# The down product of an ffn as seven half products

## The chip, the core and the metric

The kernel runs on one core of a Trainium2 chip. The number is device time in microseconds (us) of one execution, lower is better. TensorE multiplies 128x128 tiles into PSUM banks of 512 float32 columns; VectorE, ScalarE and GpSimd work on SBUF (GpSimd not on PSUM); SyncE issues the transfers between HBM and SBUF.

## The reference, cut to what matters

Two transformer blocks on 1024 tokens of width 1024. The change lies in the last part of the first block:

```python
u = rmsnorm(h, ffn_norm_pre)
gt = causal_dwconv(u @ ffn_w_gate, ffn_conv_w, ffn_conv_b)          # 1024 -> 2816
y = (gelu(gt) * (u @ ffn_w_up)) @ ffn_w_down                        # 2816 -> 1024
h = h + rmsnorm(y, ffn_norm_post)
```

The product with `ffn_w_down` is [1024 tokens, 2816] x [2816, 1024]. Everything is float32. A float32 product is made of three fp32r ones: each operand is split into a rounded high part and the rest (low), and high x high, high x low and low x high are added in PSUM.

## The kernel before, in words

The kernel is a row of stages; each is a block in which the five engines run their own lists of instructions, joined by semaphores, with a barrier at its end. Two stages matter here.

`stage_ffn` (L1329) makes the inner rows, tile by tile (22 tiles of 128 features, `KF` = 22), and SyncE stores each to HBM (`hid_d`, "inner_scratch", L1417). Tiles 3 to 20 are made with seven half products in place of eight (`seven`, L1508): sums of weights by VectorE (`combine`, L1762), high parts by ScalarE (L1595), low parts of weights by GpSimd (L1442). The last tile is plain: TensorE's last matmuls there are L1582, then VectorE multiplies (`multiply(KF - 1)`, L1849, L1759) and SyncE stores. Near its end SyncE loads the first two K tiles of the down weights and of the rows (L1431, L1434), ScalarE makes the first high part (L1676), GpSimd its low part (L1466).

`stage_down` (L1852) computes the down product transposed: the output is 8 tiles of 128 features by 1024 tokens, in two halves of 512 tokens. In a half all eight banks (one for each output tile) gather over the 22 K tiles. A step is one K tile: SyncE loads 128 weight rows of 1024 (L1875) and 128 inner rows of 512 tokens (L1877), two steps ahead; ScalarE casts the high parts (L1950, L1951); VectorE subtracts the low parts (L1924, L1925), and `lo_made` releases TensorE's 8 x 3 matmuls (L1892 to L1894); the end of the step (`used`) releases ScalarE's next cast. Between the halves VectorE copies the banks to `y` (L1930), and TensorE's second half waits for each bank's copy (L1890). ScalarE squares `y` (L1959), GpSimd adds the squares into `acc` (L1987), and TensorE multiplies by ones for the sums over features (L1913, L1915). The next stage (`stage_in2`, L1998) starts with the inverse root of these sums (L2200); `end_part` (L3957) clears semaphores between them.

## Time and profile before

| | |
|---|---|
| median of 3 runs | 2900.97 us (2899.46 to 2901.78) |
| the profiled execution | 2906.65 us, its span 2904.6 us |
| TensorE matmuls busy over the span | 2715.2 us (93%) |
| VectorE, ScalarE, GpSimd busy | 1827.6, 1249.0, 655.7 us |
| the ffn stage's seven-product tiles | 19.4 us each, 18 of them |
| the down stage, first to last matmul | 1254.9 to 1505.1 us of the span |

A line of the profile's order of time gives the start, the duration, the engine, the line, the operation with the tiles it writes and reads, its count, and in brackets how long the engine had been idle before it and what ended that. TensorE's matmuls overlap, so a matmul's duration is longer than the distance to the next; the distances give the pace. The granted clock (PEclk) is a share of full speed.

### The profile page before, as it was taken

The page shows a single profiled execution, that of the slowest core. Times are in us where ns is not written, and L with a number is a line of the kernel's source. Part 1 is how long each engine was busy: PE and PEld are TensorE (multiplying, and loading weights), DVE is VectorE, ACT ScalarE, POOL GpSimd, SP SyncE. Part 2 cuts the span into 40 slices and gives each one's busy share as a digit, 9 for nine tenths or more (in the row PEclk, how much of TensorE's full clock was granted, in tenths as well). Part 3 has the DMA queues.
Part 4 walks back from the last instruction along what each step waited for, and adds up shares of the span by engine and source line. Part 5 has one row for each costly group of instructions (what it writes and reads, how often), then busy time and mean ns, then how long its engine had stood idle before and what let it go on. Part 6 is the DMA issues. An engine that isn't in the chain of part 4 may idle for free. (4 is left out here: it accounts for less than half of the span.)

```text
span 2904.6 us, 38465 instructions
## 1 busy us (share of the span) xinstructions
PE 2715.2 (93%) x14472; PEld 2350.3 (81%) x14472; DVE 1827.6 (63%) x2284; ACT 1249.0 (43%) x1870; POOL 655.7 (23%) x406
## 2 busy tenths in 40 slices
PE   8989999999879999999989998889998999999993
PEld 7989999899768888878767888667786688888882
DVE  5366655462487777733434733765354899999996
ACT  4342333332333233222334213654333477777773
POOL 3000000002165555500110000003510144444441
PEclk9999999999999999999989999889998999999997
DMA  5343233343212222235432211113303599999996
GB/s 190 99 130 99 85 102 99 120 141 128 87 44 66 88 87 69 92 115 196 140 99 87 52 58 59 44 44 109 94 25 131 215 416 420 414 416 412 416 414 236
DMA packets 254404, 460.34 MB, mean 158 GB/s; under 512 B 22818, under 2 KB 181810, under 8 KB 229186
## 3 DMA queue, kind: packets, MB, share of 16 engines
q1 hardware_dynamic: 244770, 423.95, 40.7%
q0 software_dynamic: 9504, 34.61, 3.0%
q8 instruction: 88, 1.44, 0.2%
q14 instruction: 42, 0.34, 0.0%
HBM read 387.08 MB, written 71.43 MB: 158 GB/s over the span
## 5 line engine op out<-in xcount | busy, mean ns | idle before, releaser
L3889 DVE TENSOR_TENSOR k_w_lo<-k_raw,k_w_hi 128x2048 fp32r<-128x2048 f32 x192 | 433.6, 2288 | 34.5 <-ACT k_w_hi L3825 30.9
L3825 ACT CAST k_w_hi<-k_raw 128x2048 fp32r<-128x2048 f32 x192 | 363.1, 1911 | 64.4 <-PE bank L3743 41.3
L120 PE MATMUL bank<-u_hi,p_w_hi 128*128 128x342 f32 (+2 forms) x720 | 237.8, 330 | 8.9 <-DVEq L889 6.0
L121 PE MATMUL bank<-u_lo,p_w_hi 128*128 128x342 f32 (+2 forms) x720 | 231.9, 322 | 0.0
L122 PE MATMUL bank<-u_hi,p_w_lo 128*128 128x342 f32 (+2 forms) x720 | 231.6, 322 | 0.0
L3741 PE MATMUL bank<-k_w_hi,k_x_hi 128*128 128x512 f32 x512 | 203.0, 397 | 1.3 <-DVE k_x_lo L3895 1.0
L3743 PE MATMUL bank<-k_w_hi,k_x_lo 128*128 128x512 f32 x512 | 199.8, 390 | 0.0
L3742 PE MATMUL bank<-k_w_lo,k_x_hi 128*128 128x512 f32 x512 | 199.3, 389 | 0.0
L1471 PE MATMUL bank<-u_ffn_hi,f_w_hi 128*128 128x512 f32 (+3 forms) x520 | 171.4, 330 | 17.6 <-DVE f_inner L1759 8.4
L1472 PE MATMUL bank<-u_ffn_lo,f_w_hi 128*128 128x512 f32 (+3 forms) x520 | 167.7, 323 | 0.0
L1473 PE MATMUL bank<-u_ffn_hi,f_w_lo 128*128 128x512 f32 (+3 forms) x520 | 167.4, 322 | 0.0
L1924 DVE TENSOR_TENSOR f_w_lo<-d_raw,f_w_hi 128x1024 fp32r<-128x1024 f32 x43 | 53.6, 1247 | 156.5 <-ACT d_x_hi L1951 156.5
L1892 PE MATMUL bank<-d_x_hi,f_w_hi 128*128 128x512 f32 x352 | 139.5, 396 | 8.4 <-DVE qa L1930 4.5
L120 PEld LDWEIGHTS bank<-u_hi,p_w_hi 128*128 128x128 f32 x720 | 136.9, 190 | 9.4 <-DVEq L889 6.3
L1044 POOL TENSOR_TENSOR f_w_lo<-d_raw,f_w_hi 128x1024 fp32r<-128x1024 f32 x2 | 5.0, 2499 | 611.3 <-ACT f_w_hi L1117 611.3
L1442 POOL TENSOR_TENSOR f_w_lo<-f_raw,f_w_hi 128x512 fp32r<-128x512 f32 x66 | 107.6, 1632 | 141.2 <-ACT f_w_hi L1595 141.2
L1893 PE MATMUL bank<-d_x_lo,f_w_hi 128*128 128x512 f32 x352 | 139.1, 395 | 0.0
L1894 PE MATMUL bank<-d_x_hi,f_w_lo 128*128 128x512 f32 x352 | 138.8, 394 | 0.0
L121 PEld LDWEIGHTS bank<-u_lo,p_w_hi 128*128 128x128 f32 x720 | 137.0, 190 | 0.0
L122 PEld LDWEIGHTS bank<-u_hi,p_w_lo 128*128 128x128 f32 x720 | 136.7, 190 | 0.0
L857 DVE COPY_PREDICATED h_scores<-level,bank 128x512 f32<-128x512 int32 x72 | 53.3, 741 | 128.9 <-PE bank L769 102.6
L1442 POOL TENSOR_TENSOR f_w_lo<-d_raw,f_w_hi 128x512 fp32r<-128x512 f32 x72 | 104.5, 1453 | 84.9 <-ACT f_w_hi L1595 84.8
(606 smaller groups left out, 7354.9 us busy)
## 6 DMA issues: line engine op xcount, KB each, us to landing
k_raw<-in_w_e_gate_dram SPq DMA_DIRECT2D x64, 1024.0 KB, 7.0
k_raw<-in_w_e_up_dram SPq DMA_DIRECT2D x64, 1024.0 KB, 7.6
k_raw<-in_w_e_down_dram SPq DMA_DIRECT2D x64, 1024.0 KB, 8.2
d_raw<-in_ffn_w_down_dram SPq DMA_DIRECT2D x44, 512.0 KB, 3.6
p_w<-in_w_in_dram SPq DMA_DIRECT2D x34, 512.0 KB, 4.4
f_raw<-in_ffn_w_gate_dram SPq DMA_DIRECT2D x22, 512.0 KB, 3.7
f_raw<-in_ffn_w_up_dram SPq DMA_DIRECT2D x22, 512.0 KB, 4.9
inner_scratch<-f_inner SPq DMA_DIRECT2D x22, 512.0 KB, 5.5
```

What stands on the lines that cost most here:

```text
L120: pe.matmul(out, wh[:, t, :], xh[t][:, c:c + n], start=t == 0, stop=False)
L121: pe.matmul(out, wh[:, t, :], xl[t][:, c:c + n], start=False, stop=False)
L122: m = pe.matmul(out, wl[:, t, :], xh[t][:, c:c + n], start=False, stop=t == tiles - 1)
L1442: pool.tensor_tensor(ring(wl, q), operand(q)[0], ring(wh, q), ALU.subtract).then_inc(lo_made, 1)
L1471: pe.matmul(out, ring(wh, q)[:, k, :], xh, start=first, stop=False)
L1472: pe.matmul(out, ring(wh, q)[:, k, :], xl, start=False, stop=False)
L1473: return pe.matmul(out, ring(wl, q)[:, k, :], xh, start=False, stop=last)
L3741: pe.matmul(out, hi, wh[:, q, col], start=first, stop=False)
L3742: pe.matmul(out, hi, wl[:, q, col], start=False, stop=False)
L3743: return pe.matmul(out, lo, wh[:, q, col], start=False, stop=last)
L3825: act.copy(wh[:, q, :], raw[:, r, :]).then_inc(hi_made, 1)
L3889: dve.tensor_tensor(wl[:, q, :], raw[:, r, :], wh[:, q, :], ALU.subtract).then_inc(lo_made, 1)
```

## The change

The down product is written as a 2x2 block product: K in two halves of 11 tiles (the first digit of a weight block's name and of a row block's), output features in two halves of 512 (the second digit of the weights'), tokens in two halves of 512 (the second digit of the rows'). It is made with seven products of half size in turn instead of eight. A product multiplies one sum or single block of weights by one of rows (`COMBOS`), in 11 steps of 4 x 3 matmuls, into four banks; the other four are emptied meanwhile. VectorE makes the sums, and the rows' low parts; the weights' low parts are made by VectorE in products 0, 1 and 6 and by GpSimd in 2 to 5. Results are added and subtracted in `y` by VectorE (`fold`), after a copy by ScalarE where a quarter of `y` is written first. Block 11 of the weights and of the rows is loaded once into kept buffers, later block 00. Operands have rings of 4 (weights, loads) and 5 (rows). Steps 0 and 1 are made ready in `stage_ffn`, whose last multiply and store move to `stage_down`. `h` is loaded by tiles in product 5. Twelve of the sixteen squares are added by GpSimd during the product, the last four by TensorE. The sums' banks are 4 and 5 now. The loops are unrolled. The diff is cut to its core; of `stage_down` the new lists are shown, and the class `Down` holds the rings, the loads and the splits.

```diff
                 if n == KF - 1:
-                    sp.wait_ge(lo_made, first_operand(KF - 1))
-                    for s in range(2):
-                        sp.dma_start(down_raw[:, s, :], A["ffn_w_down"][0][s * P:(s + 1) * P, :]).then_inc(down_in[s], 16)
-                    for s in range(2):
-                        sp.wait_ge(hid_out[s], 16)
-                        sp.dma_start(down_x[s], hid_d[s][:, 0:BANK]).then_inc(down_in[s], 16)
+                    raw_read(sp, n - 1)
+                    sp.wait_ge(pmm, PRODUCTS * len(FAST) - 1)
+                    down.load(sp, 0)
+                    down.load(sp, 1)
                 store(n - 1)
-            store(KF - 1)
+            raw_read(sp, KF - 1)
+            down.load(sp, 2)
+            down.load(sp, 3)
...
             keep_gate(KF - 1)
-            act.wait_ge(down_in[0], 32)
-            act.copy(wh[:, 1, :, :].rearrange("p k n -> p (k n)"), down_raw[:, 0, :]).then_inc(down_hi, 1)
-            gelu(KF - 1)
+            for step in range(2):
+                down.weights_high(act, step)
+                down.rows_high(act, step)
+            act.wait_ge(conv3, KF)
+            act.activation(part[:, (KF - 1) % 2, 0:SEQ], part[:, (KF - 1) % 2, 0:SEQ], ACT.Gelu_apprx_tanh).then_inc(down.tail_gelu, 1)
...
             multiply(KF - 2)
+            dve.wait_ge(lo_made, first_operand(KF - 1))
+            down.sums(dve, 0)
+            down.sums(dve, 1)
             conv(KF - 1)
-            multiply(KF - 1)
+            for step in range(2):
+                down.weights_low(dve, step)
+                down.rows_low(dve, step)
...
+HALF_K = KF // 2
+COMBOS = (
+    (("10", "11", ALU.subtract), ("10", "11", ALU.add)),
+    (("00", "11", ALU.add), ("00", "11", ALU.add)),
+    (("00",), ("01", "11", ALU.subtract)),
+    (("00", "10", ALU.add), ("11",)),
+    (("11",), ("10", "00", ALU.subtract)),
+    (("01", "11", ALU.add), ("00",)),
+    (("01", "00", ALU.subtract), ("00", "01", ALU.add)),
+)
+KEPT_W = ("11",) * 6 + ("00",)
+KEPT_X = ("11",) * 4 + ("00",) * 3
+STEPS = PRODUCTS * HALF_K
+LOW_BY_DVE = (0, 1, 6)
...
+    def transfers(self, step):
+        i, j = divmod(step, HALF_K)
+        at = 0
+        out = []
+        for name in COMBOS[i][0][:2]:
+            if name != KEPT_W[i]:
+                out.append((self.piece(step, at), self.weights(name, j)))
+                at += 1
+        for name in COMBOS[i][1][:2]:
+            if name != KEPT_X[i]:
+                out.append((self.piece(step, 1), self.rows(name, j)))
+        if i == 0:
+            out.append((self.kept_w[j], self.weights(KEPT_W[0], j)))
+            out.append((self.kept_x[j], self.rows(KEPT_X[0], j)))
+        if i == 4:
+            out.append((self.kept_x[j], self.rows(KEPT_X[4], j)))
+        ahead = step - (5 * HALF_K + 5)
+        if 0 <= ahead < HALF_K:
+            out.append((self.kept_w[ahead], self.weights(KEPT_W[6], ahead)))
+        return out
...
+    def weights_ready(self, engine, step):
+        made = self.w_lo_dve if self.by_dve(step) else self.w_lo_pool
+        engine.wait_ge(made, sum(self.by_dve(n) == self.by_dve(step) for n in range(step + 1)))
+
+    def load(self, sp, step):
+        if step >= 4:
+            self.weights_ready(sp, step - 4)
+            sp.wait_ge(self.x_lo, step - 3)
+        if step < HALF_K:
+            n = HALF_K + step
+            sp.wait_ge(self.hid_out[n % 2], 16 * (n // 2 + 1))
+        for to, source in self.transfers(step):
+            sp.dma_start(to, source).then_inc(self.w_in[step % 4], 16)
...
+    def sums(self, dve, step):
+        i = step // HALF_K
+        dve.wait_ge(self.w_in[step % 4], self.landed(step))
+        if self.is_sum(step, 0):
+            a, b, op = COMBOS[i][0]
+            if step >= 2:
+                self.weights_ready(dve, step - 2)
+            dve.tensor_tensor(self.t[step % 2], self.weight_source(a, i, step, 0), self.weight_source(b, i, step, 1), op).then_inc(self.t_made, 1)
+        if self.is_sum(step, 1):
+            a, b, op = COMBOS[i][1]
+            if step >= 2:
+                dve.wait_ge(self.x_lo, step - 1)
+            dve.tensor_tensor(self.s[step % 2], self.row_source(a, i, step), self.row_source(b, i, step), op).then_inc(self.s_made, 1)
...
+        if step >= 4:
+            act.wait_ge(self.used, step - 3)
+        elif step >= 2:
+            act.wait_ge(self.tail_mm, 1)
+        act.copy(self.ring(self.wh, step).rearrange("p k n -> p (k n)"), self.weight_raw(step)).then_inc(self.w_hi, 1)
...
+        if step >= 5:
+            act.wait_ge(self.used, step - 4)
+        act.copy(self.xh[step % 5], self.row_raw(step)).then_inc(self.x_hi, 1)
...
+    def weights_low(self, engine, step):
+        made = self.w_lo_dve if self.by_dve(step) else self.w_lo_pool
+        engine.wait_ge(self.w_hi, step + 1)
+        engine.tensor_tensor(self.ring(self.wl, step).rearrange("p k n -> p (k n)"), self.weight_raw(step),
+                           self.ring(self.wh, step).rearrange("p k n -> p (k n)"), ALU.subtract).then_inc(made, 1)
+
+    def rows_low(self, dve, step):
+        dve.wait_ge(self.x_hi, step + 1)
+        dve.tensor_tensor(self.xl[step % 5], self.row_raw(step), self.xh[step % 5], ALU.subtract).then_inc(self.x_lo, 1)
...
+            d.load(sp, 4)
+            d.load(sp, 5)
+            sp.wait_ge(tail_made, 2)
+            sp.dma_start(d.hid_d[KF - 1], part[:, last, 0:SEQ]).then_inc(d.hid_out[last], 16)
+            for step in range(6, STEPS):
+                if step == HALF_K:
+                    sp.wait_ge(d.hid_out[0], 16 * HALF_K)
+                d.load(sp, step)
+                k = step - 5 * HALF_K
+                if 0 <= k < KD:
+                    sp.dma_start(h[:, k, :], h_load[:, k, :]).then_inc(h_in, 16)
+            sp.wait_ge(h_in, 16 * KD)
...
+            for step in range(STEPS):
+                i, j = divmod(step, HALF_K)
+                wh, wl = d.ring(d.wh, step), d.ring(d.wl, step)
+                xh, xl = d.xh[step % 5], d.xl[step % 5]
+                d.weights_ready(pe, step)
+                pe.wait_ge(d.x_lo, step + 1)
+                for p in range(4):
+                    if j == 0:
+                        free_bank(i, p)
+                    out = bank_of(i, p)[:, :]
+                    pe.matmul(out, wh[:, p, :], xh, start=j == 0, stop=False)
+                    pe.matmul(out, wh[:, p, :], xl, start=False, stop=False)
+                    m = pe.matmul(out, wl[:, p, :], xh, start=False, stop=j == HALF_K - 1)
+                    if j == HALF_K - 1:
                         m.then_inc(mm, 1)
+                if j < HALF_K - 1:
+                    m.then_inc(d.used, 1)
                 else:
+                    pe.wait_ge(mm, 4 * (i + 1))
+                    pe.sem_inc(d.used, 1)
+            pe.wait_ge(added, 12)
+            pe.wait_ge(folded, 28)
             for half in range(2):
+                pe.matmul(bank[4 + half][:, :], K["ones"][:, :], acc[:, half * BANK:(half + 1) * BANK], start=True, stop=half == 0)
+            for p in range(4):
+                pe.wait_ge(squared, 12 + p + 1)
+                pe.matmul(bank[5][:, :], K["ones"][:, :], sqs[:, p, :], start=False, stop=p == 3)
...
+            dve.wait_ge(d.tail_gelu, 1)
+            dve.wait_ge(d.tail_mm, 1)
+            for j, (c, w) in enumerate(SEQS):
+                half = part[:, last, c:c + w]
+                dve.tensor_tensor(half, half, bank[UP_LAST[j]][:, 0:w], ALU.mult).then_inc(tail_made, 1)
+            for step in range(2, STEPS + 1):
+                if step < STEPS:
+                    d.sums(dve, step)
+                if step > 2:
+                    if d.by_dve(step - 1):
+                        d.weights_low(dve, step - 1)
+                    d.rows_low(dve, step - 1)
+                i, j = divmod(step, HALF_K)
+                if 4 <= j < 8 and i:
+                    evict(i - 1, j - 4)
+            for p in range(4):
+                evict(PRODUCTS - 1, p)
...
+            for step in range(2, STEPS):
+                d.weights_high(act, step)
+                d.rows_high(act, step)
+                i, j = divmod(step, HALF_K)
+                if 4 <= j < 8 and i in (1, 2, 3, 5):
+                    c, t = {1: (0, 0), 2: (1, 1), 3: (0, 1), 5: (1, 0)}[i]
+                    copy(c, t, j - 4, i - 1)
+                if 7 <= j and i in (4, 5, 6):
+                    square(4 * (i - 4) + j - 7)
+            for n in range(12, 16):
+                square(n)
...
+            for step in range(2, STEPS):
+                if not d.by_dve(step):
+                    d.weights_low(pool, step)
+                i, j = divmod(step, HALF_K)
+                if 8 <= j and i in (4, 5, 6):
+                    add(4 * (i - 4) + j - 8)
+                if j == 0 and i in (5, 6):
+                    add(4 * (i - 4) - 1)
+            add(11)
```

The folds (`evict`), by product: 1 into quarter (0, 0); 2 into (1, 1); 3 into (0, 1) and (0, 0); 4 into (0, 0); 5 into (1, 0) and (1, 1); 6 into (1, 1). Each is four instructions of 128x512 that read a bank and `y`. `raw_read`, `ring` and `hid_out` are those of `stage_ffn`.

## Rows read from the trace of the kernel before

**Rows 1.** The page's first line.
```profile
span 2904.6 us, 38465 instructions
```
**Rows 2.** Busy time by stretch: PE, PEld, DVE, ACT, POOL, PEclk, DMA share, GB/s.
```profile
1195.80:1215.20 19.40, 19.40 (x109) 17.02 (x109) 14.91 (x17) 5.86 (x11) 10.60 (x8) 1.00 0.25 82
...
1226.00:1252.00 26.00, 25.16 (x134) 22.39 (x132) 13.14 (x12) 5.45 (x8) 6.05 (x3) 1.00 0.05 21
1252.00:1380.00 128.00, 122.89 (x528) 101.11 (x528) 39.89 (x45) 35.09 (x45) 0.00 (x0) 0.97 0.52 172
```
**Rows 3.** Order of time, TensorE: down stage's start, one K tile, middle, end.
```profile
1250.77 0.39 PE L1473 MATMUL bank<-u_ffn_hi,f_w_lo 128*128 128x512 f32 x1
1254.89 0.79 PE L1892 MATMUL bank<-d_x_hi,f_w_hi 128*128 128x512 f32 x1 [3.73 <-DVE d_x_lo L1925]
...
1261.30 0.39 PE L1892 MATMUL bank<-d_x_hi,f_w_hi 128*128 128x512 f32 x1
...
1265.42 0.39 PE L1892 MATMUL bank<-d_x_hi,f_w_hi 128*128 128x512 f32 x1
...
1270.86 0.39 PE L1892 MATMUL bank<-d_x_hi,f_w_hi 128*128 128x512 f32 x1
...
1382.30 0.76 PE L1892 MATMUL bank<-d_x_hi,f_w_hi 128*128 128x512 f32 x1 [4.52 <-DVE qa L1930]
...
1504.72 0.39 PE L1894 MATMUL bank<-d_x_hi,f_w_lo 128*128 128x512 f32 x1
```
**Rows 4.** Order of time, TensorE in the ffn stage: shorter waits, what followed.
```profile
824.72 0.42 PE L1471 MATMUL bank<-u_ffn_hi,f_w_hi 128*128 128x342 f32 x1 [1.20 <-POOL u_ffn_lo L1446]
...
877.97 0.39 PE L1471 MATMUL bank<-u_ffn_hi,f_w_hi 128*128 128x258 f32 x1 [2.18 <-POOL f_w_lo L1442]
...
878.44 0.28 PE L1471 MATMUL bank<-u_ffn_hi,f_w_hi 128*128 128x258 f32 x1
...
879.65 0.42 PE L1472 MATMUL bank<-u_ffn_lo,f_w_hi 128*128 128x258 f32 x1
```
**Rows 5.** Order of time, VectorE and ScalarE at the change of stages.
```profile
1251.27 1.29 DVE L1759 TENSOR_TENSOR f_inner<-f_inner,bank 128x512 f32<-128x512 f32 x2 [4.29 <-PE bank L1473]
...
1253.49 0.62 ACT L1951 CAST d_x_hi<-f_raw 128x512 fp32r<-128x512 f32 x1 [5.42 <-SPq L1356]
```
**Rows 6.** By tile (ns: least, median, most); order of time, four back to back.
```profile
L1951 ACT CAST d_x_hi<-f_raw x44: 612/619/619, 1253.5 to 1495.2; 128x512 fp32r<-128x512 f32 x44
L1925 DVE TENSOR_TENSOR d_x_lo<-f_raw,d_x_hi x44: 681/684/1777, 1254.1 to 1497.0; 128x512 fp32r<-128x512 f32 x44
...
860.88 2.49 DVE L1727 TENSOR_TENSOR f_sums<-f_parts,f_sums 128x512 fp32r<-128x512 f32 x4
```
**Rows 7.** Order of time: VectorE beside GpSimd, reading a bank, then SBUF alone.
```profile
1221.39 0.69 DVE L1792 TENSOR_TENSOR f_parts<-bank,f_parts 128x512 f32<-128x512 f32 x1
1221.42 1.29 POOL L1442 TENSOR_TENSOR f_w_lo<-f_raw,f_w_hi 128x512 fp32r<-128x512 f32 x1 [1.43 <-ACT f_w_hi L1595]
...
1383.63 11.78 POOL L1987 TENSOR_TENSOR ka<-ka,d_sq 128x512 f32<-128x512 f32 x7
...
1387.38 1.78 DVE L1925 TENSOR_TENSOR d_x_lo<-f_raw,d_x_hi 128x512 fp32r<-128x512 f32 x1
```
**Rows 8.** Transfers: KB each and us to landing; SyncE's issue (ns); GB/s in 40 slices.
```profile
k_raw<-in_w_e_gate_dram SPq DMA_DIRECT2D x64, 1024.0 KB, 7.0
...
f_raw<-inner_scratch SPq DMA_DIRECT2D x42, 256.0 KB, 3.7
...
L1877 SPq DMA_DIRECT2D f_raw<-inner_scratch x42: 332/333/765, 1256.4 to 1487.5; - x42
...
GB/s 190 99 130 99 85 102 99 120 141 128 87 44 66 88 87 69 92 115 196 140 99 87 52 58 59 44 44 109 94 25 131 215 416 420 414 416 412 416 414 236
```
**Rows 9.** Order of time: a product with ones, and the next stage's first work.
```profile
1505.45 1.10 PE L1913 MATMUL bank<-ka,ones 128*128 128x512 f32 x2 [0.34 <-POOL ka L1987]
...
1516.12 1.26 ACT L168 ACTIVATE va<-bank,eps 128x512 f32<-128x512 f32 x2 [7.39 <-PEq L3960]
```

More of the change, by code:

```diff
@@ L1355, in stage_ffn @@
     rstd, token = g, acc
[L1356 to L1358 removed]
+    with nc.Block() as block:
         def ring(b, q):
@@ new lines, in stage_down, with quarter, bank_of @@
+def stage_down(nc, ctx, K, bank, d, part, y, acc, sqs, h, h_load):
+    mm, copied, folded, squared, added, h_in, tail_made = sems(ctx, nc, "d", "mm copied folded squared added h_in tail_made")
+    UP_LAST = (4, 5)
+    last = (KF - 1) % 2
+    def quarter(c, t, p):
+        return y[4 * c + p][:, t * BANK:(t + 1) * BANK]
+    def bank_of(i, p):
+        return bank[4 * (i % 2) + p]
+    SQUARES = tuple((c, t, p) for c, t in ((0, 1), (0, 0), (1, 0), (1, 1)) for p in range(4))
+    with nc.Block() as block:
@@ L1904, in _ @@
-                step(half, 1, 1)
-                with pe.Fori(1, PAIRS_K - 1) as i:
-                    for s in range(2):
-                        step(half, 2 * i + s, s)
-                step(half, KF - 2, 0)
-                step(half, KF - 1, 1, last=True)
-            for half in range(2):
-                pe.wait_ge(kept, KD + half + 1)
-                pe.wait_ge(added, KD if half == 0 else 2 * KD - 1)
-                pe.matmul(bank[half][:, :], K["ones"][:, :], acc[:, half * BANK:(half + 1) * BANK], start=True, stop=half == 0)
@@ L1921, in low @@
-            def low(half, k, s, made=False):
-                dve.wait_ge(hi_made, KF * half + k + 1)
-                if not made:
-                    dve.tensor_tensor(wl[:, 1 - s, :], raw[:, s, :], wh[:, 1 - s, :], ALU.subtract)
-                dve.tensor_tensor(xl[:, s, :], xr[s], xh[:, s, :], ALU.subtract).then_inc(lo_made, 1)
-            def keep(half):
-                for j in range(KD):
-                    dve.wait_ge(mm, KD * half + j + 1)
-                    dve.tensor_copy(y[j][:, half * BANK:(half + 1) * BANK], bank[j][:, :]).then_inc(kept, 1)
```

246 lines of the change are left out of this document (132 added, 114 removed).

## The prediction, made before the change was run

> **What bounds the kernel now.** The order of reading was: the span, then the busy time by stretch, then TensorE's own order of time, then the waits of the other engines around it. The profiled execution has a span of 2904.6 us [rows 1] and took 2906.65 us; the median of the runs shown is 2900.97 us. In the down stage TensorE is busy 122.9 of 128 us in the first half, VectorE 39.9, ScalarE 35.1 and GpSimd not at all [rows 2]. So TensorE bounds this stage, and its order of time says by what. Two matmuls that are one K tile (24 matmuls) apart start 5.44 us apart, which is 0.2267 us for each matmul of 512 columns [rows 3]. The stage has 22 x 8 x 3 x 2 = 1056 of them, 239.4 us at that pace. From the end of the last matmul of the stage before (1250.77 + 0.39 = 1251.16) to the end of the last one here (1504.72 + 0.39 = 1505.11) are 253.95 us [rows 3]. The 14.5 us between are two interruptions: 3.73 us idle at the start and 4.52 us at 1382.30, when the second half's banks wait for their copies [rows 3]. Behind the first one 15 matmuls take 1261.30 - 1254.89 = 6.41 us instead of 3.40, a pace of 0.427 us: this is the lower of the two clock levels (1.2 GHz), and the granted clock is 0.97 over that half [rows 2, 3]. I count 3.0 us for that after each of the two gaps; 239.4 + 3.7 + 3.0 + 4.5 + 3.0 = 253.7, so the stage is explained to 0.3 us. From 1505.11 to the first work of the next stage at 1516.12 are another 11.0 us [rows 3, 9].
>
> **Matmuls removed.** Seven products of 11 steps with 4 x 3 matmuls are 924, 132 fewer. Shape and type are as before, so 132 x 0.2267 = 29.9 us go, all of it on the path.
>
> **Start of the stage.** Before, the gap holds the barrier (ScalarE is released at 1253.49 by SyncE, about 0.6 us after the store that followed the two multiplies beginning at 1251.27) and then the cast and low part of the first rows [rows 5]. Now steps 0 and 1 are split inside the stage before, and the last multiply and store come after the barrier. TensorE waits only for the barrier: I take 0.7 us, bounds 0.5 and 1.5. What hides the moved work (four sums and four low parts on VectorE, 4.8 us, four casts on ScalarE, 2.5 us) is the end of the stage before: of its last 26 us VectorE is busy 13.1, ScalarE 5.5 and GpSimd 6.1 [rows 2]. Without that cover it would cost 4.8 us at the start. The loads of steps 0 to 3 go on SyncE's queue ahead of two stores, which nobody awaits soon. That saves 3.0 us of gap. A wait of 1.20 us was followed by no slow stretch (342 columns in 0.42 us for the first matmul, as after other waits), one of 2.18 us was followed by matmuls of 258 columns in 0.42 us instead of 0.28 [rows 4], so 0.7 us should not cost the clock and the 3.0 us of slow matmuls go as well.
>
> **Middle.** The eight copies between the halves are replaced by copies and folds of four banks at a time while the other four are filled, with eleven steps between; nothing is left to wait at. VectorE's folds of product i stand behind its low parts of step 4 and later of product i + 1, and those need operands that TensorE frees only after product i, so VectorE never waits there with something queued behind. Saved: 4.5 + 3.0 = 7.5 us.
>
> **New drains.** At each product's end TensorE waits for its own last matmul before it releases the operands. A matmul lasts 0.39 us at a pace of 0.227 [rows 3], so 0.16 us plus a semaphore; 0.2 x 6 = 1.2 us lost, bounds 0 and 0.4 x 6 = 2.4.
>
> **The first product and its transfers.** A step now lasts 12 x 0.2267 = 2.72 us, and in product 0 each step loads four pieces of 256 KB (two go to buffers kept for later): 1.05 MB in 2.72 us is 385 GB/s. The experts hold 412 to 420 GB/s [rows 8], and their 1024 KB pieces of the gate's weights (512 columns) are rows of 2 KB like these, so the rate is there, barely. The ring is tighter than the rate. Load s + 4 waits for the low rows of step s; then come four issues at 0.33 us busy each [rows 8], some 1.9 us with their spacing, and a landing of 3.7 us for one 256 KB piece alone. Then VectorE passes two rounds of four instructions before the low rows of s + 4 are there. Each takes 0.60 us back to back (four in 2.49 us, the last one's tail included) [rows 6], so 4.8 us: 1.9 + 3.7 + 4.8 + some latencies = 10.7, four steps in 10.9 us of matmuls. SyncE's one new wait, for the tail multiply, stands ahead of the store and load 6, and is over before load 5 is issued. Steps 0 to 3 are loaded before the barrier and step 2 waits for the tail multiply: 1.3 us [rows 5] and four instructions and more, ready about 5 us after the barrier, when TensorE needs it at 5.4. I follow it with pieces that queue behind each other at 2.5 us a step and find step 5 about 0.5 us late and the later ones 0.2: 1.5 us lost, bounds 0 and, with a landing of 7.0 us as the experts' 1024 KB have [rows 8], (1.9 + 7.0 + 4.8) / 4 = 3.4 us a step, 0.7 x 7 = 5 us, and with a gap that reaches 2 us another 3 for the clock: 8.
>
> **VectorE and GpSimd in each step.** In products 0, 1 and 6 VectorE has four instructions, 2.4 us of 2.72; in products 2 to 5 it has two (1.2 us) and GpSimd one of 1.29 us [rows 6, 7]. ScalarE has two of 0.62 us [rows 6], and up to two more in some steps (2.4 us): no bound. The row that matters is the meeting of the two engines. A low part of VectorE that met GpSimd's additions took 1.78 us instead of 0.68 [rows 6, 7]; one that reads a bank took 0.69 us right beside a GpSimd instruction of 1.29 us, which wasn't longer either [rows 7]. So folds are free of it, and splits and sums are not. Counted as exclusive time, products 2 and 3 need 22 x 0.62 + 11 x 1.29 = 27.8 us of 29.9, product 4 with three additions 31.7, product 5 with four 33.0. Product 6 has 44 x 0.62 = 27.3, its 8 folds 5.0, and additions of which up to 4.4 us hit: 32.3 to 36.7. That is 7.3 to 11.7 us over in products 4 to 6. The rings let VectorE lead TensorE by three steps less its own 2.7 us: 5.5 us. A tile of the ffn stage had 14.9 us of VectorE and 10.6 us of GpSimd in 19.4 us, 25.5 together, and TensorE never waited [rows 2]; this speaks for the low end. I take 3.0 us, bounds 0 and 12.7 (each event of those products adding its full 0.65 or 1.1 us to VectorE: 20.7, less 2.5 won back and 5.5 of lead). The loads of h (512 KB each, eight, in product 5) add to one or two small transfers a step and stay far under the rate; the 3 us that they could cost is inside these bounds.
>
> By the Trainium skill (SBUF — State Buffer, Who interferes with whom) a VectorE instruction with two SBUF inputs and a GpSimd instruction that reads SBUF exclude each other for a whole instruction, while one with at most one SBUF input is free. The trace agrees: 1.78 against 0.68 us, and 0.69 us for the bank's. Taken strictly it speaks against putting weights' splits on GpSimd, and its result is the first rival below.
>
> **Tail.** Before, GpSimd's backlog of additions keeps the sum product waiting 4.52 us and more. Now twelve of sixteen squares are added during the product and the last four go straight to TensorE. Six products with ones instead of three, 1.10 us each at full clock less overlap [rows 9], bounds 0.85 and 1.9, are 6.0 us; VectorE's last fold and ScalarE's last square (0.7 + 0.6) lie beside the first two. With 0.2 ahead and 1.3 behind for the stage change: 7.5 us instead of 11.0, so 3.5 saved, bounds -2 and 4.5.
>
> **Sum.** 29.9 + 3.0 + 3.0 + 7.5 + 3.5 - 1.2 - 1.5 - 3.0 = 41.2 us. The profiled execution would go from 2906.65 to 2865.5, the median from 2900.97 to 2859.8, about 2860 us.
>
> **Rivals.** (1) The two engines exclude each other and nothing overlaps: 12.7 instead of 3.0, 2869.5 us. For it: the 1.78 us row. Against: the ffn tile without a wait. Chance 0.15. (2) Product 0 is bound by its transfers: 8 instead of 1.5, 2866 us. For: 385 of 415 GB/s and a ring of four. Against: the 3.7 us landing. Chance 0.12. (3) Slower: if each VectorE instruction of products 2 to 5 meets GpSimd, a step is 2 x 1.7 = 3.4 us, and if TensorE's short waits there bring the clock down, it runs at 12 x 0.427 = 5.1 us for 44 steps: 2.4 x 44 = 106 us, 2966 us. It decides from 18 such steps on (18 x 2.4 = 43). Against: a wait of 1.20 us left the clock up [rows 4]. Chance 0.03. (4) The product is not what limits, and the time removed is waited for elsewhere (h, or code fetched for an unrolled stage): no gain, 2901 us. The ffn stage ahead is unrolled at the same density and shows no such wait [rows 2]. Chance 0.02.
>
> **How the numbers follow.** The forecast, 2860 us, has the remaining 0.68; its own range is 2853 (every loss zero) to 2866. To leave out no more than 2 in 10 the range goes to the first two rivals, and to both together, 41.2 - 9.7 - 6.5 = 25.0: 2876 us. About 0.2% (6 us) is what a measurement of this kernel can tell from no change. Faster 0.95, same 0.02, slower 0.03.
>
> **What would show it.** Matmuls at 0.227 us in all seven products; a gap under 1 us at the start with no stretch at 0.427 behind; waits on low rows in the first eleven steps of some tenths; the same on VectorE in products 4 to 6, if anywhere; 7 to 8 us from the last product to the next stage. The prediction is wrong if a gap over 2 us stands anywhere inside, or if product 0's steps take 3.4 us.

## The result and the profile after

The changed kernel took 2868.43 us (median of 4 runs, 2861.21 to 2870.06) against 2900.22 us for the kernel before in the same runs: a ratio of 0.9889, 95% interval 0.9875 to 0.9902, or 28 to 36 us less. Forecast were 2860 us and a range up to 2876; without the first two rivals it would have ended at 2866, below the measured median. The profiled execution took 2861.21 us, against the 2906.65 us of the one before [rows 1].

```profile
span 2859.5 us, 38444 instructions
```

These two profiles are 45 us apart, which is more than the change did. I measure the change on the stretch that it touches, called the stage below: from the end of the ffn's last matmul to ScalarE's first work of the next stage (L168). Before it is 1251.16 to 1516.12, 264.96 us [rows 3, 9]; after 1244.39 to 1473.07, 228.68 us. That is 36.3 us less. The other 9 us lie outside the stage, 6.8 ahead of it and some 2 behind. There the kernels differ only in the last ffn tile, where TensorE is busy throughout in both, and in where buffers lie; the times vary from execution to execution (b1_before below).

Busy time by stretch, as in [rows 2]; the stretches are an ffn tile, the ffn's end, product 0, products 1 to 5, product 6:

```profile
1195.80:1215.20 19.40, 19.40 (x110) 17.01 (x110) 13.41 (x16) 5.84 (x10) 10.49 (x8) 1.00 0.16 63
1218.40:1244.40 26.00, 25.99 (x137) 23.09 (x135) 15.21 (x18) 6.58 (x11) 3.00 (x3) 1.00 0.53 182
1244.80:1279.40 34.60, 31.61 (x133) 24.39 (x133) 28.57 (x47) 14.18 (x24) 0.00 (x0) 1.00 0.85 291
1279.40:1432.30 152.90, 151.00 (x661) 123.56 (x662) 130.19 (x153) 75.28 (x135) 75.75 (x52) 1.00 0.64 215
1432.30:1465.60 33.30, 31.08 (x132) 24.24 (x132) 31.74 (x47) 13.71 (x23) 6.40 (x4) 1.00 0.36 118
```

The granted clock is 1.00 throughout, where the first half before had 0.97 [rows 2]. The ffn's end still keeps TensorE busy 25.99 of 26 us with the first two steps' preparation in it. VectorE is busy 31.74 of 33.30 us in product 6.

TensorE's order of time, answering [rows 3]: start, the waits of product 0, two products' ends, two of the four waits of product 6, and the tail (beside [rows 9]):

```profile
1244.00 0.39 PE L1469 MATMUL bank<-u_ffn_hi,f_w_lo 128*128 128x512 f32 x1
1244.86 0.47 PE L2063 MATMUL bank<-d_x,f_w_hi 128*128 128x512 f32 x1 [0.47 <-PEq L1356]
...
1253.62 0.47 PE L2063 MATMUL bank<-d_x,f_w_hi 128*128 128x512 f32 x1 [0.31 <-DVE d_x L2006]
1257.48 0.47 PE L2063 MATMUL bank<-d_x,f_w_hi 128*128 128x512 f32 x1 [0.86 <-DVE d_x L2006]
1261.39 0.47 PE L2063 MATMUL bank<-d_x,f_w_hi 128*128 128x512 f32 x1 [0.90 <-DVE d_x L2006]
1270.30 0.47 PE L2063 MATMUL bank<-d_x,f_w_hi 128*128 128x512 f32 x1 [0.50 <-DVE d_x L2006]
...
1278.65 0.39 PE L2065 MATMUL bank<-d_x,f_w_lo 128*128 128x512 f32 x1
1279.35 0.47 PE L2063 MATMUL bank<-d_x,f_w_hi 128*128 128x512 f32 x1 [0.30 <-PE bank L2065]
...
1340.50 0.47 PE L2063 MATMUL bank<-d_x,f_w_hi 128*128 128x512 f32 x1 [0.44 <-PE bank L2065]
...
1449.22 0.47 PE L2063 MATMUL bank<-d_x,f_w_hi 128*128 128x512 f32 x1 [0.47 <-DVE d_x L2006]
1452.93 0.47 PE L2063 MATMUL bank<-d_x,f_w_hi 128*128 128x512 f32 x1 [0.72 <-DVE d_x L2006]
...
1466.02 1.95 PE L2076 MATMUL bank<-mixed_squares,ones 128*128 128x512 f32 x4 [0.34 <-DVE vm L2084]
```

The two long interruptions are gone: 0.47 us at the start where 3.73 stood, nothing in the middle where 4.52 stood. In their place are many short ones of three kinds. At 1279.35 and 1340.50 TensorE waits for its own last matmul. The waits up to 1270 lie in product 0, those from 1449 on in product 6, both on VectorE's low parts. What VectorE itself waits for in product 0 (what, for whom, us in total, times, longest) is a transfer:

```profile
DVE d_raw L1971 <- DMA d_kept<-inner_scratch: 5.9, 5, 1.4
```

From a product's first matmul to the next one's, with 132 x 0.2267 = 29.92 us as the least (all 924 matmuls are in these traces). Product 6 is taken to the start of its last matmul and 0.2267 us more. Tail is from the end of the last matmul to L168, and whole time the median of the runs with the ratio's 95% interval to the kernel before in the same runs:

```
kernel          product 0  products 1 to 5               6      tail  stage   whole time, ratio
before          -          -                             -      11.0  264.96  2900.97
b1_before       -          -                             -      10.8  264.45  2896.63, 0.9975 to 1.0
changed         34.49      30.51 30.64 30.62 30.47 30.60 33.34  7.38  228.68  2868.43, 0.9875 to 0.9902
e1_again        35.35      30.47 30.62 30.59 30.49 30.61 33.54  7.35  229.65  2868.36, 0.9862 to 0.9898
e2_no_drain     32.63      29.92 29.92 29.92 29.92 29.92 34.78  6.80  224.45  2864.10, 0.9853 to 0.9886
e3_early        33.59      30.49 30.59 30.58 30.48 30.59 33.86  7.35  228.16  2865.16, 0.986 to 0.9893
e4_no_adds      35.37      30.51 30.62 30.59 30.49 30.61 31.90  7.06  227.78  2866.80, 0.985 to 0.989
e5_all_dve      34.18      30.49 30.60 30.58 30.47 30.64 33.40  7.06  228.05  2863.61, 0.9849 to 0.9899
e6_all_pool     33.55      32.46 32.34 30.58 30.51 31.13 33.33  7.06  231.59  2868.79, 0.9871 to 0.9918
e7_three        33.07      29.92 29.92 29.92 29.92 29.92 35.25  6.52  225.08  2859.85, 0.9845 to 0.9889
e8_store_late   32.11      30.48 30.60 30.58 30.47 30.59 34.66  7.38  227.50  2866.99, 0.9865 to 0.9919
e9_dve_alone    32.71      29.92 29.92 29.92 29.92 29.92 32.58  6.51  222.04  2856.13, 0.9837 to 0.9871
e10_h_ahead     32.26      29.92 29.92 29.92 29.92 29.92 32.16  6.51  221.20  2857.31, 0.984 to 0.9868
e11_gap         35.03      30.48 32.98 32.22 30.47 30.62 33.28  7.35  233.06  2865.40, 0.9853 to 0.9901
```

The intervals of the whole time are some 10 us wide and most overlap; the causes are therefore read from the product lengths, which agree to 0.1 us in products 1 to 5. Product 0 agrees less: changed, e1_again, e4_no_adds, e5_all_dve and e11_gap have the same code there and take 34.18 to 35.37 us.

### The profile page after: what moved, and what is told of

Its sections match the earlier page's. It is cut to its first block and busy times, and to the rows that moved or that the text cites. A ratio compares the mean times of both kernels' runs of the same rounds, so it can differ in the third digit from the quotient of the medians.

```text
span 2859.5 us, 38444 instructions
## 1 busy us (share of the span) xinstructions
PE 2677.1 (94%) x14346; PEld 2315.4 (81%) x14346; DVE 1927.9 (67%) x2433; ACT 1276.8 (45%) x1952; POOL 711.8 (25%) x446
## 5 line engine op out<-in xcount | busy, mean ns | idle before, releaser
L4008 ACT CAST k_w_hi<-k_raw 128x2048 fp32r<-128x2048 f32 x192 | 363.1, 1912 | 64.2 <-PE bank L3926 41.2
L2063 PE MATMUL bank<-d_x,f_w_hi 128*128 128x512 f32 x308 | 121.2, 394 | 7.5 <-DVE d_x L2006 5.2
L3883 POOL DMA_INDIRECT y_scratch<-k_y,k_to x32 | 73.8, 2308 | 213.9 <-POOLq L3881 213.9
L1467 PEld LDWEIGHTS bank<-u_ffn_hi,f_w_hi 128*128 128x128 f32 x520 | 99.9, 192 | 27.5 <-issue 14.4
L2065 PE MATMUL bank<-d_x,f_w_lo 128*128 128x512 f32 x308 | 120.0, 390 | 0.0
```

Source lines behind the costliest of these rows:

```text
L1467: pe.matmul(out, ring(wh, q)[:, k, :], xh, start=first, stop=False)
L4008: act.copy(wh[:, q, :], raw[:, r, :]).then_inc(hi_made, 1)
```

## Experiments

### The same two kernels again

b1_before is the kernel before, e1_again the changed kernel, each unchanged.

> The kernel before once more, to see how much of the difference between two profiled executions lies outside the down stage. Its first profile has 265.0 us from the last ffn matmul to the next stage's first work. Theory A (the stage is the same each time): 265 within 1 us again, so the stage saves 35 to 36 us, and what is left over, up to 6 us either way, is spread elsewhere. Theory B (the first profile had an unusually slow stage): 262 or less, which would bring the stage's saving to the 32 us of the medians.

> The changed kernel again, to tell the stage's saving from what differs between executions. From the end of the last ffn matmul to the first work of the stage after the down product the changed kernel's profile has 228.7 us, the kernel before 265.0: 36.3 us saved there, while the two profiled executions differ by 45 us and the medians by 32. Theory A (the stage is the same in each execution, the rest is spread of stages that were not touched): again 228.7 within 1 us, and a time ratio of 0.987 to 0.990. Theory B (the stage itself varies, since its short waits sometimes bring the clock down): another stage length, 232 us or more, with a stretch of matmuls 0.427 us apart.

The stages are 264.45 and 229.65 us, 34.8 apart after 36.3 in the first pair: each is within 1 us of the first time. What lies ahead of the stage moves more: it begins at 1251.16 and 1242.99 us in the two executions of the kernel before and at 1244.39 and 1249.83 in those of the changed one, so both have both. One place of it can be named, the wait on GpSimd in the ffn of [rows 4], which in both kernels is 2.1 to 2.2 us in the late executions and 1.0 to 1.1 in the early ones; totals of TensorE's waits in the ffn, the kernel before first and b1_before second:

```profile
PE bank L1471 <- POOL f_w_lo L1442: 2.2, 1, 2.2
```
```profile
PE bank L1471 <- POOL f_w_lo L1442: 1.0, 1, 1.0
```

Behind the longer wait (2.10 to 2.18 us in before, e1_again, e2_no_drain and e5_all_dve) 15 matmuls of 258 columns start 0.21 to 0.22 us apart; behind the shorter one (0.98 in b1_before, 1.06 in the changed kernel) all keep their 0.12. That is some 1.5 us more, and with the wait it covers the 2.2 us that arise in the ffn between the two executions of the kernel before. The other 6.0 of their 8.2 us are there already at the ffn's first matmul (774.0 and 768.0) and were not followed.

Inside the stage the two interruptions are not the same twice. Starts of TensorE's matmuls in b1_before, each gap and the first matmul back at full pace:

```profile
1246.72 0.75 PE L1892 MATMUL bank<-d_x_hi,f_w_hi 128*128 128x512 f32 x1 [3.73 <-DVE d_x_lo L1925]
...
1250.24 0.40 PE L1894 MATMUL bank<-d_x_hi,f_w_lo 128*128 128x512 f32 x1
...
1373.79 0.77 PE L1892 MATMUL bank<-d_x_hi,f_w_hi 128*128 128x512 f32 x1 [5.46 <-DVE qa L1930]
...
1379.90 0.40 PE L1894 MATMUL bank<-d_x_hi,f_w_lo 128*128 128x512 f32 x1
```

Behind the same 3.73 us of gap as before, 8 distances take 3.52 us, which is 1.7 us lost to slow matmuls instead of 3.0; behind the second gap, 5.46 us for 4.52, 14 take 6.11, 2.9 us lost instead of 2.5. All four together are 13.8 us here and 13.7 in the first execution: the sums agree although the parts do not.

### The drain between products

```diff
-                else:
-                    pe.wait_ge(mm, 4 * (i + 1))
-                    pe.sem_inc(d.used, 1)
```

ScalarE, which is what that signal releases, waits for `mm` itself at those steps.

> TensorE no longer waits for its own last matmul at a product's end; the operands of that step are released to ScalarE by the semaphore of its last matmuls themselves. In the changed kernel's profile products 1 to 5 last 30.5 to 30.6 us instead of 29.9. Theory A (the 0.6 us is this drain: about 0.4 idle and 0.2 of lost overlap): products 1 to 5 last 29.9 to 30.0, the stage 225.0, 3.7 us less. Theory B (the 0.6 us belongs to the change of banks or to operands that come late): products last 30.5 as before and the stage keeps 228.7.

Products 1 to 5 fall from 30.47 to 30.64 to exactly 29.92 each. The boundary of products 0 and 1 has no mark of its own in TensorE's order of time of e2_no_drain:

```profile
1284.23 0.39 PE L2073 MATMUL bank<-d_x,f_w_lo 128*128 128x512 f32 x1
1284.46 0.39 PE L2071 MATMUL bank<-d_x,f_w_hi 128*128 128x512 f32 x1
1284.68 0.39 PE L2072 MATMUL bank<-d_x,f_w_hi 128*128 128x512 f32 x1
```

So a drain costs 0.55 to 0.72 us. Starts are 0.70 us apart at 1278.65 in the changed kernel's rows above and the next two (1279.35 and 1279.65) 0.30 apart, in place of twice 0.227. Of these 0.55 us 0.30 are the idle time in brackets, 0.16 the unfinished end of the last matmul, and the rest the slower first one. Where the idle time is 0.41 or 0.44 the whole is 0.67 to 0.72. The six idle times are 2.2 us together. Six drains are 3.8 us, and a seventh stands ahead of the tail (6.80 instead of 7.35). But product 6 grows from 33.3 or 33.5 to 34.8: a part of what TensorE wins it loses to VectorE there.

### Product 0: releasing loads earlier, and the store

e3_early releases the loads by the sums that consumed the piece, and no longer by the low parts made from them:

```diff
-            self.weights_ready(sp, step - 4)
-            sp.wait_ge(self.x_lo, step - 3)
+            for side, made, low in ((0, self.t_made, None), (1, self.s_made, self.x_lo)):
+                if self.is_sum(step - 4, side):
+                    sp.wait_ge(made, self.count(step - 4, side))
```

(where a side is a single block, the old wait stays). e8_store_late has this and moves the store of the ffn's last row from behind load 5 to behind load 7.

> A load's buffer is released by the sums that read it, where both operands of the step are sums (products 0, 1 and 6), not by the low parts made one round later: 2.4 us and more earlier. In the changed kernel product 0 lasts 34.5 us, of which 29.9 are matmuls and 0.6 its drain. Theory A (the ring's round trip of issue, landing and two rounds of VectorE is what is late): product 0 comes to 30.5 to 31.5 us, the stage to 225.2. Theory B (the transfers' rate, 1.05 MB in each 2.72 us, is what is late): product 0 keeps 34 us or more, its transfers at 400 GB/s before and after.

> Loads released by the sums, as in the run before of that kind, and besides the store of the last inner row (512 KB) is issued behind the loads of step 7 instead of step 5. In that run TensorE still waited 1.62 us at step 4 or 5 and 0.90 us at the next, and while the store was under way the transfers moved 180 to 260 GB/s at a busy share of 0.84 to 0.87. Theory A (the store takes transfer time from the loads of steps 5 and 6): these waits fall to under 1 us together, product 0 from 33.6 to 32 us or less, as far as step 10, which needs the stored row, isn't late then. Theory B (the loads of steps 4 and 5 are late because they start only after the barrier, whatever follows them): the 1.6 us wait stays.

In e3_early the waits of the later steps are gone and the two early ones stay as they were, so it lands between its two theories; e8_store_late shrinks those to 0.8 us together, as its theory A had it. TensorE's waits in product 0, e1_again, e3_early and e8_store_late:

```profile
1263.02 0.47 PE L2063 MATMUL bank<-d_x,f_w_hi 128*128 128x512 f32 x1 [1.56 <-DVE d_x L2006]
1266.92 0.47 PE L2063 MATMUL bank<-d_x,f_w_hi 128*128 128x512 f32 x1 [0.92 <-DVE d_x L2006]
1276.10 0.47 PE L2063 MATMUL bank<-d_x,f_w_hi 128*128 128x512 f32 x1 [0.76 <-DVE d_x L2006]
1279.56 0.47 PE L2063 MATMUL bank<-d_x,f_w_hi 128*128 128x512 f32 x1 [0.49 <-DVE d_x L2006]
```
```profile
1263.25 0.47 PE L2068 MATMUL bank<-d_x,f_w_hi 128*128 128x512 f32 x1 [1.62 <-DVE d_x L2011]
1267.13 0.47 PE L2068 MATMUL bank<-d_x,f_w_hi 128*128 128x512 f32 x1 [0.90 <-DVE d_x L2011]
```
```profile
1262.06 0.47 PE L2069 MATMUL bank<-d_x,f_w_hi 128*128 128x512 f32 x1 [0.22 <-DVE d_x L2011]
1271.07 0.47 PE L2069 MATMUL bank<-d_x,f_w_hi 128*128 128x512 f32 x1 [0.58 <-DVE d_x L2011]
```

The stage begins at the same time in both (1249.97 and 1249.96). Busy time by stretch of e3_early, then of e8_store_late (DMA share and GB/s are the last two):

```profile
1254.00:1258.00 4.00, 4.00 (x19) 3.34 (x18) 3.27 (x7) 1.93 (x4) 0.00 (x0) 1.00 0.86 220
1258.00:1270.00 12.00, 9.48 (x41) 7.13 (x41) 8.34 (x14) 3.67 (x6) 0.00 (x0) 1.00 1.04 402
```
```profile
1254.00:1258.00 4.00, 4.00 (x19) 3.34 (x18) 3.02 (x6) 1.74 (x4) 0.00 (x0) 1.00 0.88 274
1258.00:1270.00 12.00, 11.78 (x51) 9.17 (x51) 9.80 (x17) 4.71 (x9) 0.00 (x0) 1.00 1.05 406
```

In the first four microseconds shown, the transfers move 220 GB/s with the 512 KB store among them and 274 without; both have 402 or 406 afterwards. The store itself does not lower the rate: e8_store_late issues it at 1258.66, and the transfers move 405 GB/s from there to 1262.70. What it takes is its own 512 KB, and with the store moved TensorE's wait at step 4 falls from 1.62 to 0.22 us and the one at step 5 goes. Why the rate is low in those first microseconds, with the store or without, stays open.

Product 0 goes 35.35, 33.59, 32.11 in the three. Executions differ too much to give each step its price from this. The loads of e2_no_drain are those of the changed kernel, its product 0 takes 32.63 us, or some 33.2 with the drain, and it has no waits behind step 5 either. Counted with a drain, the six executions with the changed kernel's loads and store are at 33.2, 34.2, 34.5, 35.0 and twice 35.4 (e6_all_pool, whose low parts of product 0 are made elsewhere, is left out). The two with early loads (e3_early, e7_three) are at 33.6, and the three with early loads and the late store at 32.1 to 33.3. Both edits point the right way by about 1 us each; that the early release alone helps is not shown.

The early release has a limit that can be read: with it the pieces land 6.4 to 7.5 us after their issue (medians of the four kinds) where e1_again has 5.2 to 6.1, at 402 GB/s. They are issued earlier and queue longer. In e8_store_late product 6 takes 34.66 instead of 33.86: why a store in product 0 should matter there was not followed.

### Product 6: additions, lead, or VectorE itself

e4_no_adds leaves out four squares (8 to 11) and the additions in product 6, so a part of the sum of squares is missing. e5_all_dve and e6_all_pool change who makes the weights' low parts:

```diff
-LOW_BY_DVE = (0, 1, 6)
+LOW_BY_DVE = (0, 1, 2, 3, 4, 5, 6)
```
```diff
-LOW_BY_DVE = (0, 1, 6)
+LOW_BY_DVE = ()
```

> The squares of one quarter of y (features 512 to 1023, first 512 tokens) and their four additions on GpSimd are left out, so no GpSimd addition falls into product 6 from its step 8 on; the normalisation of these tokens misses half of its sum. Product 6 lasts 33.3 us in the changed kernel. Theory A (three additions hold up a VectorE instruction by 1.1 us each, 1.78 for 0.68): product 6 comes to 29.9 to 30.4, the stage to 225.4. Theory B (VectorE's four instructions a step and its eight folds alone use up its lead, 26.5 + 4.8 = 31.3 us against 29.9): product 6 keeps 31.5 us or more.

> VectorE makes the weights' low parts in all seven products, GpSimd only adds squares. Theory A (the two engines exclude each other in products 2 to 5: in the changed kernel's product 5 five VectorE instructions in a row start 1.70 us apart instead of 0.60, each beside a GpSimd one, so VectorE enters product 6 with 1.2 us of lead instead of 5.5): a step of products 2 to 5 needs three times 0.60 instead of 2 x 0.60 + 1.29 of shared time, VectorE enters product 6 three steps ahead, and product 6 comes from 33.5 to 30.5 us or less; stage 226.5 or less against 229.7 of the changed kernel run again. Theory B (VectorE has too much to do in product 6 whatever the lead): product 6 stays at 33 us or more.

> GpSimd makes the weights' low parts in all seven products. Theory A (they exclude each other): in products 0, 1 and 6 a step needs 3 x 0.60 + 1.29 = 3.1 us of shared time against 2.72, with the folds and additions of product 6 on top; product 1 comes from 30.5 to 34 us, product 6 to 36 or more, the stage to 236 to 242. Theory B (they mostly run beside each other, as in the ffn stage, where 25.5 us of both fitted into 19.4): VectorE is relieved by 0.60 us a step, product 1 stays at 30.5 and product 6 falls to 31.5 or less; stage 228.

Without the additions product 6 is 31.90 us, 1.4 to 1.6 less, so theory B holds for what remains. The waits say which steps pay for what. In the changed kernel steps 6 to 9 (counted from 0) wait, here only 6 and 7:

```profile
1457.17 0.47 PE L2063 MATMUL bank<-d_x,f_w_hi 128*128 128x512 f32 x1 [0.60 <-DVE d_x L2006]
...
1460.78 0.47 PE L2063 MATMUL bank<-d_x,f_w_hi 128*128 128x512 f32 x1 [0.60 <-DVE d_x L2006]
```

These two starts are 3.61 us apart, where twelve matmuls need 2.72. The eight folds stand in steps 4 to 7, two in each, so VectorE has six instructions of 0.60 us there. The additions hit the steps behind. Folds spread over more steps of product 6 were not tried.

With VectorE making all low parts product 6 stays at 33.40, though GpSimd is then no longer beside VectorE in products 2 to 5, but for the additions. VectorE has the first operands of product 6 ready 2.1 us before TensorE starts it, instead of 1.2, and the order of time of VectorE in e5_all_dve shows where the gain is spent, on a transfer that comes late early in product 6:

```profile
1440.42 0.68 DVE L2006 TENSOR_TENSOR d_x<-d_raw,d_x 128x512 fp32r<-128x512 f32 x1
1442.10 0.69 DVE L1971 TENSOR_TENSOR d_raw<-f_raw,d_kept 128x512 f32<-128x512 f32 x1 [1.00 <-DMA d_kept<-in_ffn_w_down_dram]
```

In the changed kernel the lead goes at the end of product 5. GpSimd (low part, addition, low part, additions) and VectorE there:

```profile
1420.14 1.73 POOL L2001 TENSOR_TENSOR f_w_lo<-d_raw,f_w_hi 128x512 fp32r<-128x512 f32 x1
1421.84 1.74 POOL L2162 TENSOR_TENSOR mixed_squares<-mixed_squares,f_parts 128x512 f32<-128x512 f32 x1
...
1420.65 1.78 DVE L2006 TENSOR_TENSOR d_x<-d_kept,d_x 128x512 fp32r<-128x512 f32 x1
1422.35 1.78 DVE L1971 TENSOR_TENSOR d_raw<-f_raw,d_kept 128x512 f32<-128x512 f32 x1
1424.05 1.78 DVE L1976 TENSOR_TENSOR d_raw<-d_kept,f_raw 128x512 f32<-128x512 f32 x1
```

Each VectorE instruction is 1.70 us behind the one before instead of 0.60 [rows 6], and each has one of GpSimd beside it: while both have work, they take turns.

e6_all_pool is the dearest of these three, but cheaper than its theory A: 231.59 us of stage where 236 to 242 was expected, and product 6 stays at 33.33. Product 1, whose steps then have three instructions of VectorE and one of GpSimd, takes 32.46 us; product 2, whose steps are those of the changed kernel, takes 32.34 because VectorE enters it late and its folds come on top. VectorE and GpSimd in product 1:

```profile
1289.28 1.78 DVE L1971 TENSOR_TENSOR d_raw<-f_raw,d_kept 128x512 f32<-128x512 f32 x1
1290.98 0.68 DVE L1976 TENSOR_TENSOR d_raw<-f_raw,d_kept 128x512 f32<-128x512 f32 x1
1291.59 0.68 DVE L2006 TENSOR_TENSOR d_x<-d_raw,d_x 128x512 fp32r<-128x512 f32 x1
1292.19 1.77 DVE L1971 TENSOR_TENSOR d_raw<-f_raw,d_kept 128x512 f32<-128x512 f32 x1
```
```profile
1288.88 1.63 POOL L2001 TENSOR_TENSOR f_w_lo<-d_raw,f_w_hi 128x512 fp32r<-128x512 f32 x1 [1.28 <-ACT f_w_hi L1987]
```

A step is 1292.19 - 1289.28 = 2.91 us, against 2.72 of matmuls and 2.4 with all four instructions on VectorE. One instruction given to GpSimd delays VectorE by 1.1 us to spare it 0.6. By the Trainium skill (SBUF — State Buffer, Who interferes with whom) the second of the two engines is blocked for the whole of the other's instruction. The trace agrees: the VectorE instruction that starts inside GpSimd's (1289.28, after 1288.88) is 1.1 us longer, the two after it have their 0.68.

### A gap put back

In the middle of the old stage stood a gap and slow matmuls behind it. e11_gap makes TensorE wait, ahead of product 3, for the low parts of three steps later:

```diff
-                d.weights_ready(pe, step)
-                pe.wait_ge(d.x_lo, step + 1)
+                ahead = 3 if step == 3 * HALF_K else 0
+                d.weights_ready(pe, step + ahead)
+                pe.wait_ge(d.x_lo, step + ahead + 1)
```

> The changed kernel, with one gap put back in the middle: before the first matmul of product 3 TensorE waits for the low parts of the step three further on. In the changed kernel these were ready at about 1342.8 us, and the last matmul of product 2 ended at 1340.06: a gap of some 2.8 us where 0.44 stood, 2.4 us more. It prices the 6 us of the prediction that were put down to slow matmuls behind the two old gaps. Theory A (such a gap costs the clock as well): the matmuls behind it start 0.43 us apart in place of 0.227 for some 15 of them, product 3 takes 30.6 us and up to 3.0 more, and the stage 228.7 + 2.4 + 3.0 = 234.1, less what product 6 gives back because VectorE enters it with a longer lead (up to 3 us). Theory B (the clock stays up after one gap of this length): all matmuls of product 3 at 0.227 us, and only the 2.4 us appear, with the same amount given back in product 6.

```profile
1343.31 0.47 PE L2064 MATMUL bank<-d_x,f_w_hi 128*128 128x512 f32 x1 [2.79 <-DVE d_x L2006]
...
1347.22 0.43 PE L2065 MATMUL bank<-d_x,f_w_hi 128*128 128x512 f32 x1
```

The gap is 2.79 us, as expected. Behind it two starts come at 0.30 and 0.23 us, the next eight distances are 0.39 to 0.43 (1343.84 to 1347.22), then 0.227 again. Product 2 grows by 2.3 us with the gap and product 3 by 1.6 with the slow matmuls, and nothing comes back in product 6 (33.28). Theory A has the mechanism, with 1.6 us in place of "up to 3.0". Before, the same count is 13 behind the gap of 3.73 (3.0 us with the first matmul's) and 10 behind that of 4.52 (2.5 us); in b1_before it is 7 behind 3.73 (1.7 us) and 13 behind 5.46 (2.9 us). So these gaps brought slow matmuls, but their length doesn't say how many. Every gap up to 1.62 us in these stages was followed by none, and so was one of 2.25 us near the end of product 6 in e6_all_pool (at 1468.92). The whole time, 2865.4 us, shows none of these 4 us: that is how little it resolves.

### A version that beats both

e7_three is e2_no_drain, e3_early and e5_all_dve together. e9_dve_alone adds the later store and gives all additions of squares to VectorE, so GpSimd has nothing to do in the stage; e10_h_ahead also loads `h` in product 2, not 5.

```diff
+            def add(n):
+                ...
+                    dve.tensor_tensor(to, to, sqs[:, n % 4, :], ALU.add).then_inc(added, 1)
...
-                k = step - 5 * HALF_K
+                k = step - 2 * HALF_K
```

> Three edits together: no drain at the products' ends, loads released by the sums, and the weights' low parts all on VectorE. If the three losses are separate, the stage goes from 229.7 us by 3.7 to 4.5, by about 1.5 and by 3: to 221 us, with products 1 to 6 at 29.9 each, and the time to about 2860 us. If they only hand the same wait on (a faster TensorE meets VectorE's limit sooner, as product 6 at 35.0 us showed without the drains), the stage ends at 223.5 or more.

> The three edits of the run before (no drains, early loads, all low parts on VectorE), the store of the last inner row behind the loads of step 7, and the twelve additions of squares on VectorE too, so GpSimd has nothing in this stage. Theory A (a GpSimd addition costs VectorE 1.1 us, its own addition 0.6 us, and VectorE is the bound of product 6): product 6 needs 26.5 + 4.8 + 4 x 0.6 = 33.7 us of VectorE and enters with more lead, so it comes from 35.3 to 31 to 33 us; product 0 to 31.5; stage 220 to 222, time about 2857 us. Theory B (moving additions to VectorE only adds to the engine that is the bound): product 6 stays at 35 us or more.

> As the run with GpSimd idle, and besides h is loaded by tiles in product 2 instead of product 5, so that these 4 MB no longer lie between the loads that product 6 waits for. With all low parts on VectorE one VectorE instruction of product 6 waited 1.0 us for a kept block. Theory A (that wait reaches TensorE): product 6 is 1 us shorter than in the run beside it. Theory B (it is hidden): no difference within 0.3 us.

e7_three has the best products 1 to 5 and the longest product 6, 35.25 us, and its stage of 225.08 us is the second case of what was expected: a faster TensorE meets VectorE's limit sooner. With the additions on VectorE and the later store product 6 is 2.7 us shorter, within theory A's 31 to 33; the store alone did not shorten it above, so I put this down to the additions, though no run has them alone. Busy time of product 6 in e9_dve_alone:

```profile
1427.60:1460.20 32.60, 31.33 (x134) 24.40 (x133) 29.73 (x49) 13.03 (x22) 0.00 (x0) 1.00 0.35 113
```

The stage is 222.04 and 221.20 us, some 7 less than the changed kernel's 228.68 and 229.65, and the whole time 2856.13 and 2857.31 against 2868.4; of these 12 us the stage explains 7, and the rest is not explained. Between e9_dve_alone and e10_h_ahead the runs don't decide (product 6 is 0.4 us shorter, between the two theories). About 5 us stay in product 0 and product 6 together, the latter bound by VectorE's 2.4 us of 2.72 a step and its folds.

## Why the prediction held, point by point

The median of 2868.43 us is above the 2866 at which the forecast's own range ended; it is inside the full range because that was widened for rivals 1 and 2. (With every loss zero the sum is 46.9 and gives 2854 us, not 2853.) The mechanism held; two terms of the sum, the drains and product 0, were too small.

**Matmuls, 29.9.** Right: without drains five products take exactly 132 x 0.2267 us.

**Start, 3.0 and 3.0.** Right: 3.73 became 0.47 (3.3 us), the slow matmuls went (3.0 us in the trace the prediction was made from, 1.7 in b1_before), and the ffn's end bore the moved work without a wait.

**Middle, 7.5.** Nearly: 4.52 of gap and 2.5 of slow matmuls, 7.0; in b1_before 5.46 and 2.9, 8.4. I had taken the first gap's 3.0 for the second. The side remark that VectorE never waits there with something queued behind was wrong. Its folds wait for ScalarE's copies; the totals in products 1 to 5 of the changed kernel include

```profile
DVE vm L2084 <- ACT qa L2131: 6.0, 4, 2.5
```

It cost TensorE nothing there.

**Drains, 1.2.** The step that failed in size: 3.8 us, beyond the bound of 2.4. I counted 0.16 us for the unfinished end of the last matmul, which is right, and 0.04 for the semaphore. TensorE stands idle for 0.30 to 0.44 us between the end of that matmul and the next one's start, and the first matmul after a stop costs about 0.1 more.

**Product 0, 1.5.** 4.0 and 4.9 us beyond the drain, inside the bounds (0 to 8), two and a half times the value taken. The issues (four to a step) and a landing of 3.7 us for a piece alone did not describe pieces under load: the medians of the four kinds are 3.5 to 5.4 us in the changed kernel's product 0 and up to 6.1 in e1_again's. I had also passed over the store, noting only what it waits for and not what its 512 KB take from the loads. The release by the low parts may have cost as well; the runs do not show it apart from the spread of product 0. Rival 2 was partly right: with an earlier release the pieces queue longer, at 402 GB/s.

**VectorE and GpSimd, 3.0.** 3.4 us, all in product 6. The size was right and the reasoning not, so that the number fits is luck. The "lead of 5.5 us" was not there: at the end of product 5 the engines take turns, and about 1.2 us were left. And I had the additions as the main cost, while they are 1.5 of 3.4 us; the rest is VectorE's own work, 44 x 0.60 + 8 x 0.60 = 31.2 us ahead of any meeting, more than TensorE's 29.9, and bunched: 3.6 us a step where the folds are. Exclusion itself holds wherever both have SBUF work, as rival 1 said, but in products 2 to 5 VectorE has room for it.

**Tail, 3.5.** 11.0 became 7.38: 3.6.

Together: 29.9 + 3.3 + 3.0 + 7.0 + 3.6 - 3.8 - 4.0 - 3.4 = 35.6 us where the stage shows 36.3. In the second pair, 29.9 + 3.3 + 1.7 + 8.4 + 3.5 - 3.8 - 4.9 - 3.6 = 34.5 where it shows 34.8. The forecast's 41.2 is too high mainly by the drains (2.6) and product 0 (2.5 to 3.4). The median fell by 31.8, less than the stage in either pair; the interval (28 to 36) reaches about to both, and whether the untouched parts lose 3 us or the medians differ by chance stays open.

## What to carry to other kernels

A wait of TensorE for its own last matmul costs more than the idle time in brackets shows: six such waits were 2.2 us idle and 3.8 us lost, the rest being the overlap of matmuls on both sides of the stop. A stream of loads sized near the transfer rate must be checked with every store that shares it, above all where the first loads are already late. Work that one engine does in bunches must be counted in the steps where it stands: VectorE's average fitted almost, its 3.6 us in the steps with folds did not. Moving an instruction from VectorE to GpSimd helps only if it lies beside instructions of VectorE that read a bank or beside idle time; here it cost VectorE 1.1 us to be spared 0.6.

## What the runs showed of the hardware that I had not expected

A wait of TensorE for its own last matmul costs 0.55 to 0.72 us with matmuls 0.227 us apart, 0.30 to 0.44 of it as idle time. The stretch at the lower clock is not fixed by the gap ahead of it: 8 slow distances after 2.79 us, 10 after 4.52, 13 after 5.46, and after the same 3.73 us 13 in one execution and 7 in another of the same kernel. A gap of 2.1 to 2.2 us in the ffn was followed by 15 slow matmuls of 258 columns in four executions, one of 1.0 to 1.1 us by none in two, and one of 2.25 us in e6_all_pool's product 6 by none. The transfers moved 220 to 274 GB/s in product 0's window from 1254 to 1258 us, with the 512 KB store and without it, and 405 GB/s later with the same store among them.
